# Two transformer blocks in split fp32 on one core: the residual stream, gate, up and MLP products turned so that the weight tile is stationary

## The reference, cut to what matters

```python
def rms_norm(x, w):                       # w: one gain per feature
    y = x * lax.rsqrt(jnp.mean(x * x, axis=-1, keepdims=True) + EPS)
    return y * w
for layer in range(2):                    # first block
    u = rms_norm(x, attn_norm_w[layer]) @ w_in[layer]            # 1024 x 2560
    ...                                   # retention or differential attention, memory attention
    x = x + mixed @ w_out[layer]                                 # 1024 x 1024
    gu = rms_norm(x, ffn_norm_w[layer]) @ w_gate_up[layer]       # 1024 x 5632
    x = x + (silu(gu[..., :2816]) * gu[..., 2816:]) @ w_down[layer]   # 2816 x 1024
# second block
proj = rmsnorm(x, norm_mix_g) @ w_in_2                           # 1024 x 9232
...                                       # gated delta rule, gated linear attention
x = x + merged @ w_out_2
q = rmsnorm(x, norm_xattn_g) @ xattn_wq
...
x = x + o @ xattn_wo
x = x + square(relu(rmsnorm(x, norm_mlp_g) @ mlp_w1)) @ mlp_w2   # 1024 x 4096, 4096 x 1024
return rmsnorm(x, norm_final_g)
```

## Time and profile before

| | |
|---|---|
| median of 3 runs | 1475.19 us (1475.12 to 1476.76) |
| profiled execution | 1472.4 us, span 1471.1 us |
| PE busy | 1371.4 us (93%), 6640 records |
| weight loads (PEld) | 1116.9 us (76%) |
| DVE, ACT, POOL busy | 851.7, 690.7, 167.3 us |
| mean granted TensorE clock | 0.968 |
| DMA | 222 MB, mean 151 GB/s |

### The profile page before, as it was taken

One profiled execution on the slowest core, in us unless ns is written; L12 is line 12 of the kernel. 1 busy time (PEld: TensorE's weight loads), 2 busy tenths in 40 slices (PEclk: granted clock), 3 DMA queues, 4 the chain that ended last, 5 costly groups with the idle time before them and its releaser, 6 DMA issues.

```text
span 1471.1 us, 16590 instructions
## 1 busy us (share of the span) xinstructions
PE 1371.4 (93%) x6640; PEld 1116.9 (76%) x6640; DVE 851.7 (58%) x1107; ACT 690.7 (47%) x991; POOL 167.3 (11%) x142
## 2 busy tenths in 40 slices
PE   5998999999989899999988998899989889999997
PEld 4887788887767678888766886797757677788886
DVE  5555755557664465555558657744754554554453
ACT  4563544445665444444356245424653336454442
POOL 1101000002200010000003311422131000011100
PEclk9999999999999799999999999999999989999999
DMA  7646466655445455666433313314434533365551
GB/s 287 216 143 187 141 195 201 190 174 176 144 142 172 127 165 174 196 199 196 136 86 115 87 58 87 114 44 109 116 105 161 196 115 129 115 227 173 186 188 69
DMA packets 118445, 222.23 MB, mean 151 GB/s; under 512 B 8225, under 2 KB 53409, under 8 KB 118369
## 3 DMA queue, kind: packets, MB, share of 16 engines
q1 hardware_dynamic: 114448, 206.60, 44.3%
q0 software_dynamic: 3056, 11.89, 2.4%
q10 hardware_dynamic: 864, 2.69, 0.5%
HBM read 218.00 MB, written 3.15 MB: 150 GB/s over the span
## 4 chain that ended last, share of the span: by engine, by line
PE 76%; DVE 13%; ACT 6%; issue 2%; POOL 1%; DMA 1%; ACTq 0%; DVEq 0%
PE ps L318 21%; PE ps L320 20%; PE ps L319 20%; DVE spl L1267 3%; ACT spl L896 2%; PE ps L336 2%; DVE ar L1522 2%; POOL sml L1785 1%; PE ps L671 1%; PE ps L666 1%; PE ps L646 1%; DVE ar L1560 1%; DVE ar L1287 1%; DVE sml L1306 1%; PE ps L729 1%
## 5 line engine op out<-in xcount | busy, mean ns | idle before, releaser
L1267 DVE TENSOR_TENSOR spl<-raw,spl 128x1024 fp32r<-128x1024 f32 x388 | 475.1, 1247 | 192.0 <-ACT spl L896 190.5
L896 ACT CAST spl<-raw 128x1024 fp32r<-128x1024 f32 x388 | 400.8, 1048 | 216.7 <-PE ps L320 141.4
L318 PE MATMUL ps<-spl,xs 128*128 128x512 f32 x1056 | 430.3, 408 | 8.7 <-DVE xs L1294 8.3
L319 PE MATMUL ps<-spl,xs 128*128 128x512 f32 x1056 | 418.3, 396 | 0.0
L320 PE MATMUL ps<-spl,xs 128*128 128x512 f32 x1056 | 417.7, 396 | 0.0
L318 PEld LDWEIGHTS ps<-spl,xs 128*128 128x128 f32 x1056 | 203.0, 192 | 55.9 <-DVE xs L1294 11.4
L320 PEld LDWEIGHTS ps<-spl,xs 128*128 128x128 f32 x1056 | 202.5, 192 | 44.2
L319 PEld LDWEIGHTS ps<-spl,xs 128*128 128x128 f32 x1056 | 203.2, 192 | 39.3
L318 PE MATMUL ps<-spl,ys 128*128 128x512 f32 x496 | 201.8, 407 | 5.3 <-DVE spl L1267 3.0
L320 PE MATMUL ps<-spl,ys 128*128 128x512 f32 x496 | 196.2, 395 | 0.0
L319 PE MATMUL ps<-spl,ys 128*128 128x512 f32 x496 | 195.8, 395 | 0.0
(11 more groups left out here) (283 smaller groups left out, 1232.5 us busy)
## 6 DMA issues: line engine op xcount, KB each, us to landing
raw<-in_w_in SPq DMA_DIRECT2D x112, 512.0 KB, 3.7
raw<-in_w_gate_up SPq DMA_DIRECT2D x176, 256.0 KB, 4.2
raw<-in_mlp_w SPq DMA_DIRECT2D x64, 512.0 KB, 4.3
raw<-in_w_down SPq DMA_DIRECT2D x44, 512.0 KB, 4.1
raw<-in_w_out SPq DMA_DIRECT2D x24, 512.0 KB, 4.1
ar<-in_gains POOLq DMA_DIRECT2D x9, 512.0 KB, 5.9
raw<-in_w_mem_kv SPq DMA_DIRECT2D x8, 512.0 KB, 6.1
raw<-in_xattn_wk SPq DMA_DIRECT2D x8, 512.0 KB, 4.0
```

Source lines behind the costliest of these rows:

```text
L318: self.do.matmul(bank, xh, hi, start=start, stop=False)
L319: self.do.matmul(bank, xh, lo, start=False, stop=False)
L896: self.do.copy(self.k.spl[:, u % NH, 0, :], self.k.raw[:, u % NR, :]).then_inc(*self.up("hi", (u,)))
L1267: self.do.tensor_tensor(lo, self.k.raw[:, u % NR, :], hi.bitcast(F32), ALU.subtract).then_inc(*self.up("lo", (u,)))
```

## The change

`X` is replaced by `XT`, features on partitions (128 x 8 feature tiles x 256 tokens). The products `w_out` (both layers), `w_out_2`, `xattn_wo`, `w_gate_up`, `w_down` and `mlp_w1` use a turned product: a 128 x 128 tile of the weight is stationary, and 256 tokens of the activation move. `w_in`, `w_in_2`, the memory and attention keys and values, both branch products, `xattn_wq` and `mlp_w2` keep the old form.

```diff
+    def product_turned(self, u, x, kt, hi, lo, out, start, stop, *keys):
+        xh, xl = x[:, 0, kt, :], x[:, 1, kt, :]
+        self.wait_ge(*self.at("hi", u))
+        self.do.matmul(out, hi, xh, start=start, stop=False)
+        self.do.matmul(out, hi, xl, start=False, stop=False)
+        self.wait_ge(*self.at("lo", u))
+        m = self.do.matmul(out, lo, xh, start=False, stop=stop)
...
+    def squares_sum(self, n):
+        s = self.s(f"sqa_{n}")
+        b = self.hold("sum", n)
...
+        self.wait_ge(*self.at("pm", "sum", n))
+        for t in range(2):
+            m = self.do.matmul(b[:, t:t + 1], s[:, t * P:(t + 1) * P], self.ones()[:, 0:1], start=True, stop=True)
...
-    def ffn_turn(self, l, b):
-        s = self.s2(f"act{b}")
-        bk = self.hold("ft", l, b)
...
-    def mlp_turn(self, b, t):
...
+    def norm_tiles(self, n, acc):          # VectorE
+        x = self.k.x["xs"]
+        for p in range(5):
+            if p < 4:
+                v = self.k.XT[:, 2 * p:2 * p + 2, :]
+                self.wait_ge(*self.at("mm", acc, p))
+                self.do.tensor_tensor(v, self.psg(2, acc, p), v, ALU.add).then_inc(*self.up("rx", ("x", n, p)))
+            if p:
+                for kt in (2 * p - 2, 2 * p - 1):
+                    self.wait_ge(*self.at("xh", n, kt))
+                    self.do.scalar_tensor_tensor(x[:, 1, kt, :], self.k.XT[:, kt, :], self.gain(n, kt),
+                                                 x[:, 0, kt, :].bitcast(F32), ALU.mult,
+                                                 ALU.subtract).then_inc(*self.up("xl", (n, kt)))
...
+    def norm_tiles(self, n, acc):          # GpSimd
+        a, b = self.s(f"sqa_{n}"), self.s(f"sqb_{n}")
+        for i, v in enumerate((a, b)):
+            self.wait_ge(*self.at("sq", n, 2 * i + 1))
+            self.do.tensor_tensor(v[:, 0:512], v[:, 0:512], v[:, 512:1024], ALU.add).then_inc(*self.up("pm", ("s", n, i)))
...
-            E.rows(("fd", l), wd, range(2 * b + n0, 2 * b + n0 + g), n0, 2, "ys", 2 * (b % 4), lambda t, kt: ("xl", "ft", l, b),
...
+    for n0, g in ((0, 1), (1, 1), (2, 1), (3, 1), (4, 1), (5, 3)):
+        E.rows_turned(acc, w, range(n0, n0 + g), n0, 8, "ys", 0, ready, True, True, acc)
```

More of the change, by code:

```diff
@@ L230, in cS, with ones, gain, r @@
         return self.k.con[:, 256:384]
[L232 to L266, removed]
-            self.ahead(0)
-            self.need(pre, 1, 0)
-            self.need(pre, 1, 1)
-            self.after(pre)
-    def rows(self, acc, w, kts, n0, nk, xin, off, ready, first, last, done, pre=None):
-        self.u += len(kts)
-        if pre:
-            for t, j in TK:
-                self.need(pre, t, j)
-    def spread(self, n, src, dst, free=()):
-        self.norms[n] = (None, src, dst, None, free)
+    def ones(self):
+        return self.k.con[:, 1408:1536]
+    def gain(self, n, kt):
+        return self.V("gain", 8 * GAINS.index(n) + kt)
+    def r(self, n, t):
+        return self.small(f"r_{n}", 2)[:, t:t + 1]
+    def cols(self, blk, src, k0, xin, ready, release="ev"):
+        self.u += 1
+    def cols_turned(self, blk, src, k0, xin, n):
+        self.u += 1
+    def rows(self, acc, w, kts, n0, nk, xin, off, ready, first, last, done):
+        self.u += len(kts)
+    def rows_turned(self, acc, w, kts, n0, nk, xin, off, ready, first, last, done):
+        self.u += len(kts)
+    def spread(self, n, src, dst):
+        self.norms[n] = (src, dst)
     def group_rs(self, tag, v, n, w, scale, eps, *ready, mul=None):
@@ new lines, in factor_rows, with cols @@
+    def factor_rows(self, n):
+        d = self.s(f"rb_{n}")[:, 512:768]
+        b = self.hold("rb", n)
+        self.wait_ge(*self.at("dm", "diag", n))
+        for t in range(2):
+            m = self.do.matmul(b[:, t * P:(t + 1) * P], self.ones(), d[:, t * P:(t + 1) * P], start=True, stop=True)
+        m.then_inc(*self.up("mx", ("rb", n)))
+        self.let(("rb", n), "am", "rb", n)
+    def cols(self, blk, src, k0, xin, ready, release="ev"):
+        x = self.k.x[xin]
+        u, hi, lo = self.next_unit(src(k0))
@@ L1963, in block, with norm, norm_factor, norm_rows @@
         yield
[L1966 removed]
+def norm(E, n, acc):
+    E.take(f"sqa_{n}", f"sqb_{n}")
+    E.norm_tiles(n, acc)
+    E.acc_done(acc, n)
+    E.ahead()
+def norm_factor(E, n):
+    E.squares_sum(n)
+    E.give(f"sqa_{n}", ("mx", "sum", n))
+    E.give(f"sqb_{n}", ("pm", "sum", n))
+def norm_rows(E, n):
+    E.take(f"rb_{n}")
+    E.factor_rows(n)
+def residual(E, acc, w, ready, n, spread=None):
+    if spread:
+        E.turn(spread, 0, 0)
+        E.turn(spread, 1, 0)
+    for n0, g in ((0, 1), (1, 1), (2, 1), (3, 1), (4, 1), (5, 3)):
+        E.rows_turned(acc, w, range(n0, n0 + g), n0, 8, "ys", 0, ready, True, True, acc)
+        if spread and n0 < 2:
+            E.turn(spread, n0, 1)
+        if g == 1:
+            E.ahead()
+    norm(E, n, acc)
+def branch(E, acc, w, xin, ready, groups):
     n0 = 0
     for g in groups:
[L1970 removed]
+        E.rows(acc, w, range(n0, n0 + g), n0, 8, xin, 0, ready, True, True, acc)
         n0 += g
```

687 lines of the change are left out of this document (371 added, 316 removed).

## The result

The changed kernel takes **1499.84 us** (median of four runs, 1498.61 to 1504.23), the kernel before beside it 1475.97: ratio 1.0164, 95% interval 1.014 to 1.0189. It is 1.6% slower; the forecast was 1442, 2.3% faster, with a range up to 1467. The profiled execution took 1499.5 (span 1498.0).

What follows compares the result with a forecast made beforehand. PE was taken as the bound. Terms 7.1 - 17.0 - 28.3 + 5.8 + 5 - 6 = -33.4 took the profiled 1472.4 us to 1439.0; with the median 2.8 higher, forecast 1442 us, range 1425 to 1467.

Steps and rivals of the forecast that it cites:

- Pitch of the turned products: Turned products: 4704 matmuls of 256 columns at 115 ns replace 2352 of 512 at 227 ns, +7.1 us.
- rival 1: Turned matmuls: the extra 13.4 ns are a fixed price of each, so 120.1 ns and 1466 us; chance 14%.
- Blocks: Feed-forward and MLP blocks: four transposes of 0.446 us go from each of 38 places, -17.0 us.
- Norms and new waits: Six norms: lost PE time and transposes go, -28.3 us; new waits for square sums and factors, +5 (0 to 15).
- the small matmuls: Added on PE: six pairs of one-column matmuls, 2.7 us, and three pairs for factor rows, 1.3 us.
- Nothing is late at this place: Products after the norms: feature tiles are ready when PE arrives, so no wait was counted.
- Rival 4: New norm and feed-forward chains late: 2 us lost at each, waits 15 not 5, 1452 us; chance 10%.
- Added on PE: 16 transposes back, one-column matmuls for the sums and matmuls for factor rows, +5.8 us.
- the start: Kernel start: no gain row needed, x transposed inside kv0; 3 us saved at first product, 3 behind kv0, -6 (-2 to -8).
- Rival 2: Turned matmuls: weight load and stream share reads, 136 ns each, 1541 us; 11%, including any other pitch over 122 ns.
- Rival 3: Turned matmuls: the weight load holds the pitch at 112 ns, giving 1428 us; chance 12%.
- Rival 5: Norm boundaries not saved because a bank or half-buffer is released late: 28 us come back, 1470 us; chance 3%.

Runs made afterwards that it cites:

- e3: Kernel before, nothing turned, with two matmuls of 256 columns for one of 512 in every product that the change turns: 1505.00 us, ratio 1.0204.
- p1: Probe kernel by itself: fp32r matmul pitch at 512 to 64 moving columns (256: 120 ns), and POOL's 512-column add alone (1.29 us) and beside DVE (up to 2.2).
- e5: Kernel e1 with gate and up products put back to the old form, w_down still turned: 1463.89 us, ratio 0.9921.
- e1: Changed kernel with the four adds of squares moved from POOL to DVE: 1468.68 us, ratio 0.9957.
- p5: Probe kernel: POOL's second add at 24 starts, DVE's run headed by a PSUM add (5.46 to 5.77 us) or a 256-column operation (at most 2.4).
- e8: Changed kernel with POOL's first add of each norm waiting until DVE's last add to XT is done: 1494.74 us, ratio 1.0135.
- p6: Probe: seven variants of DVE's work at POOL's first add (1: add only behind PSUM add; 6: DVE idles before last 256-column operation); second add up to 5.76 us.
- p2: Probe kernel: POOL's add swept over 48 starts beside DVE's four two-SBUF-input subtractions; all adds took 1.26 to 2.36 us.
- e4: Changed kernel with one small 128x2 DVE operation added between a norm's last low part and the first weight subtraction: 1500.73 us, ratio 1.0161.

## Why the prediction was wrong

It missed by 58 us (1442 against 1499.8). Two steps make nearly all of it: 23.4 in the pitch, 31.2 in POOL's adds; the rest is 3.

1. **Pitch of the turned products: wrong, mis-sized.** "I take 115 ns": measured 120, +30.5 us (e3) instead of +7.1. This was rival 1, price and time exact (120.1 ns, 31 more), with 14%. I had put it behind because of a slope in modelled ends, 0.44 ns a column, and wrote myself that it was weak; by the starts in p1 it is 106.8 / 256 = 0.417 from 256 to 512 columns, the full rate. The pitch of 512 columns was good to 0.1 ns, its split into stream and price could not be read from one width, and the change put all its weight on that split. The Trainium skill (TensorE: Matmul & The Clock Gate, "Back-to-back issue gap") gives a fixed part of 2.5 ns for a single matmul's gap, by which I estimate 109.2 ns for 256 columns, and about 131 ns per matmul for a sustained stream of 512 columns, which my prediction left out. The traces agree with neither for fp32r: the fixed part is 13.3 ns, 256 columns cost 119.9 and 512 cost 226.7 (p1).
2. **Blocks: right.** 38 x 0.446 = -17.0. A feed-forward block grew by 0.48, which is six units' pitch, 6 x 0.156 = 0.94, less 0.46; a MLP block shrank from 22.73 to 22.42, four units' 0.62 less 0.93. Together 22 x 0.46 + 8 x 0.93 = 17.5. But at 120 ns these say something the sum hid: for gate and up a block pays 0.62 to save 0.446. Turned back they gave 4.8 us (e5).
3. **Norms and new waits: the step that failed.** "PE waits 0.6 us with the third unit queued behind." I priced POOL's adds by the earlier trace rows, 1.05 and 0.6, from a kernel in which POOL's operation stood alone; and the 1.05 is a square of one tensor, while an add of two takes 1.29 even alone (p1). At four of the six norms one of them took 5.75 beside DVE's run, and the last, of 256 columns, took 1.59 at five. Over the six norms (three units before each and four behind, less their streams at full clock; worked out from starts, half clock included) PE lost in us:

```
        ffn0  attn1  ffn1  mix2  xattn  mlp   sum
before   5.0   3.2    5.0  13.0   5.8   5.1   37.1
after    9.2   4.3    8.9  18.4  10.3   8.4   59.4
e1       2.8   2.1    2.4  10.6   2.2   3.1   23.3
```

   Forecast: -28.3, +4.0 for the small matmuls, +5, so -19.3. Measured +22.2; with the adds on DVE -13.9. That leaves 5.4 us less than forecast. In e1 PE waits 1.0 at the second unit of ffn0, ffn1 and mlp for a subtraction that stands behind the norm's operations, and 0.6 at the first units of attn1 and mix2, 4.2 that I had put at nothing ("Nothing is late at this place"); the waits at sums and factor rows, 1.3 each, stay 2.4 under the 5 that I had allowed. The other 3.6 I have not traced.
4. **Rival 4 had the place, not the size.** "The sum of squares goes through four engines": 2 us a norm was foreseen, 4.6 to 4.7 came at four norms and 1.9 at two, and around each a stretch at half clock that I had not priced at all: over the launch 119 us at 1.2 GHz against 95 before, by the record of the clock.
5. **Added on PE, the start: right.** The first product starts at 10.68 instead of 13.81, and the ninth unit 7.4 us earlier than before; forecast -6, -2 to -8.
6. **Rivals 2, 3, 5 didn't happen.** The load doesn't share with the stream at 256 columns, and holds the pitch only from 224 down.

Without the pitch my terms sum to -40.5; e1 against e3, which has the new pitch and nothing else of the change, is 1468.7 - 1505.0 = -36.3. So the sum was sound beside two prices.

The Trainium skill (SBUF — State Buffer, "SBUF: two separate sides") states that a DVE operation with two SBUF inputs and a GpSimd operation that reads SBUF exclude each other for a whole instruction, whoever starts first. The traces agree wherever they take turns (p1, 2.2 us for an add, 2.3 for a subtraction). I had not weighed it for POOL's adds; with an add of 2.4 us, as p1 to p5 show where they take turns, the sum would by my estimate be ready 3.4 us earlier than it was, and the wait 1 to 2 us instead of 4.7. That a run of DVE keeps POOL out for four instructions it doesn't state.

## What to carry to other kernels

Before a product is turned or cut, count the matmuls: at 2.4 GHz each fp32r matmul of 256 columns or more costs its columns and 13.3 ns here, so going from 512 moving columns to 256 costs 6% of the product, and only what is removed beside it can pay. A POOL operation that lies on a chain is priced beside what DVE does at that instant, not by its duration where it stood alone; and letting POOL in earlier can cost DVE most of what it wins (e8). The version to keep is e5: residual stream with features on partitions, squares added on DVE, gate and up left as they were.

## What the runs showed of the hardware that I had not expected

- A DVE operation that reads PSUM, at the head of an unbroken run of DVE operations with two SBUF inputs, kept out a POOL add that came at the run's subtractions until the run was over: 4.80 to 5.77 us in 39 of 39 groups (p5, p6), and at four norms of the changed kernel. With no such operation in the run, 2.4 at most in 201 groups of p2 to p5. An add that came during the first operation behind the one that reads PSUM was let in, and the next was too: p6, variant 1 (1.27 to 1.54), attn1 and mix2 of the changed kernel, all norms of e8. Yet a turn for POOL does not always end it: in e4 at mlp the second add was let in (1.27) and the third stood for 5.62. What sets and clears this stays open; that a short idle of DVE ends it was not tested, since variant 6 missed its instant.
- The fixed 13.3 ns of a matmul show at 2.4 GHz only: at 1.2 GHz 512 columns take 426.7 ns (p1) and 256 take 0.21 us.
- fp32r matmuls with a new weight tile each start every 111 to 112 ns at 2.4 GHz, from 224 down to 64 columns, and with 64 columns every 213 ns at 1.2 GHz (p1).
- The granted clock fell to half in p1 while PE ran matmuls of 64 columns without a pause.
